# Attention's query and key projections from seven block products, weight sums by GpSimd, x loaded a second time in the merge

## The reference, cut to what matters

```
h = rms_norm(x, norm_mix)                       # 512 x 1024
proj = h @ w_in                                 # attention q, k, v; delta-rule q, k, v; gates
qa = rms_norm(q per head); ka = rms_norm(k per head); va = v      # 3 groups x 8 heads x 64
per group: dilated window attention of qa, ka, va -> output, lse
o_a = softmax over groups of lse, times the outputs
o_b = gated delta rule on (causally convolved) q, k, v
merged = sigmoid(gate_a) * (o_a @ w_branch_a) + sigmoid(gate_b) * (o_b @ w_branch_b)
x = x + merged @ w_out
```

## Time and profile before

| | |
|---|---|
| median of 3 runs | 2816.6 us |
| profiled execution | 2815.5 us |
| its span, first to last instruction | 2813.7 us |
| TensorE busy | 2726.0 us, 97% |
| VectorE, ScalarE, GpSimd busy | 46%, 21%, 0% |
| mean granted TensorE clock | 0.979 of full |
| attention, queries and keys on | 111.5 to 381 us |
| merge | 880 to 1042 us |

### The profile page before, as it was taken

The page is one execution under the profiler, slowest core; times in us unless marked ns, Lnnn a source line. Parts: engine busy times, 40 slices in busy tenths (PEclk is TensorE's granted clock), DMA queues, the critical chain, the costliest instruction groups (busy, mean ns, idle before and its releaser), DMA issues.

```text
span 2813.7 us, 29464 instructions
## 1 busy us (share of the span) xinstructions
PE 2726.0 (97%) x11558; PEld 1702.0 (60%) x11558; DVE 1282.1 (46%) x2773; ACT 580.2 (21%) x1044; POOL 0.2 (0%) x4
## 2 busy tenths in 40 slices
PE   8999989999999999999999998999999999999998
PEld 4544446676665445444444445578884484788887
DVE  1144455565552112000012585467666573777743
ACT  2145532312211001110001124221111012122201
POOL 0000000000000000000000000000000000000000
PEclk9999999999999998999999998999999999999999
DMA  4111111010011221244432220122223311222222
GB/s 184 60 60 45 53 52 44 32 45 31 31 45 60 90 82 56 92 170 171 164 119 97 75 75 1 61 83 90 79 87 119 104 49 60 77 88 90 90 90 90
DMA packets 31907, 224.74 MB, mean 80 GB/s; under 512 B 3488, under 2 KB 4128, under 8 KB 5536
## 3 DMA queue, kind: packets, MB, share of 16 engines
q1 hardware_dynamic: 30384, 219.50, 22.7%
q10 hardware_dynamic: 1392, 3.41, 0.3%
HBM read 220.80 MB, written 2.10 MB: 79 GB/s over the span
## 4 chain that ended last, share of the span: by engine, by line
PE 93%; DVE 3%; ACT 2%; issue 1%; DMA 0%; ACTq 0%; DVEq 0%
PE psum L400 91%; DVE work L2329 1%; PE psum L782 1%; PE psum L1091 0%; DVE work L709 0%; PE psum L2193 0%; PE psum L1892 0%; DVE xT L1635 0%; DVE hT L563 0%; DMA mixT<-x_dram 0%; ACT work L534 0%; PE psum L1704 0%; PE psum L3233 0%; ACT work L602 0%; ACT work L616 0%
## 5 line engine op out<-in xcount | busy, mean ns | idle before, releaser
L400 PE MATMUL psum<-hT,ring 128*128 128x512 f32 (+2 forms) x3248 | 903.3, 455 | 13.5 <-ACT work L1220 5.5
L400 PEld LDWEIGHTS psum<-hT,ring 128*128 128x128 f32 (+1 forms) x3248 | 445.7, 167 | 355.6 <-issue 324.2
L400 PE MATMUL psum<-work,ring 128*128 128x512 f32 (+1 forms) x1208 | 420.1, 499 | 8.7 <-DVE work L2391 3.9
L400 PEld LDWEIGHTS psum<-work 128*128 128x128 f32 (+2 forms) x2390 | 276.2, 178 | 113.1 <-issue 72.4
L400 PE MATMUL psum<-work 128*128 128x128 f32 (+7 forms) x2390 | 328.0, 291 | 14.3 <-ACT work L2291 11.1
L400 PEld LDWEIGHTS psum<-work,ring 128*128 128x128 f32 x1208 | 229.0, 190 | 184.7 <-issue 158.0
L400 PE MATMUL psum<-work,mixT 128*128 128x256 f32 (+2 forms) x1332 | 289.2, 379 | 2.7 <-ACT work L1745 1.5
L400 PEld LDWEIGHTS psum<-work,mixT 128*128 128x128 f32 (+1 forms) x1332 | 232.1, 182 | 49.2 <-issue 16.1
L400 PE MATMUL psum<-ring,work 128*128 (+1 forms) x568 | 247.0, 593 | 2.5 <-issue 1.9
L400 PEld LDWEIGHTS psum<-ring,work 128*128 128x128 f32 x568 | 106.7, 190 | 132.8 <-issue 129.1
L2656 DVE SCALAR_TENSOR_TENSOR work<-work,vec 128x512 f32<-128x512 f32 x176 | 125.6, 748 | 69.5 <-ACT work L2591 69.5
(11 more groups left out here) (408 smaller groups left out, 2068.1 us busy)
## 6 DMA issues: line engine op xcount, KB each, us to landing
ring<-stream_dram SPq DMA_DIRECT2D x204, 1024.0 KB, 4.8
con<-consts_dram SPq DMA_DIRECT2D x1, 2953.0 KB, 13.8
mixT<-x_dram ACTq DMA_DIRECT2D x4, 512.0 KB, 6.2
out_dram<-mixT SPq DMA_DIRECT2D x4, 512.0 KB, 3.7
work<-p_dram ACTq DMA_DIRECT2D x1, 512.0 KB, 3.9
con<-ssm_dram ACTq DMA_DIRECT2D x1, 512.0 KB, 3.5
vec<-vecs_dram SPq DMA_DIRECT2D x1, 378.0 KB, 5.5
work<-consts_dram ACTq DMA_DIRECT2D x1, 256.0 KB, 2.6
```

What stands on the lines that cost most here:

```text
L400: ins = self.eng.matmul(out, lhsT, rhs, start=start, stop=stop)
```

## The change

* Each fill's two tiles (256 output channels by 512 tokens, from 1024 input channels) are now made from seven products of blocks of 128 x 512 weights by 512 x 256 tokens, that is 28 matmuls of 256 columns in place of 16 of 512. Four sums of halves of hT are made once, by VectorE in the values stage, and kept in xT's room. Four sums of weight blocks per fill are made by GpSimd: one in a buffer of its own, three in place in the ring's slot.
* ScalarE copies three of the seven results out of PSUM, VectorE puts the two tiles together with seven additions of 256 columns, in three pieces called left, right and last; both tiles are complete only at last.
* Eleven matmuls (parts) go into each step, and the squares and head sums of both tiles of a fill come together.
* Since xT's room is taken, the turning of x moves from the values stage into the merge: x is loaded again (ScalarE's queue), and for m from 4 to 7 TensorE turns 8 blocks ahead of the gate tiles, ScalarE writes them to xT.
* ScalarE's copies of K0 and V0 move from decay_act to the end of attn_act, and TensorE's stage wait between attention and decay is dropped.
* The feed-forward's counters of h_sum start at 4 more. Nothing else of it changes.

```diff
-        TILES, AHEAD, UNITS_A, PER_STEP = 24, 6, 32, 6
+        TILES, AHEAD, UNITS_A, PER_STEP = 24, 6, 32, 11
+        SEVEN = 28
+        s_one = a(T)
+        kept = mixT[:, 0:2, :].rearrange("p a t -> p (a t)")
+        in_sums = xT[...]
+        def parts_before(n):
+            return min(SEVEN * AHEAD // 2 + PER_STEP * n, SEVEN * TILES // 2)
+        def fills_of_step(n, part):
+            at = {"left": 16, "right": 24, "last": 28}[part]
+            return [f for f in range(TILES // 2) if n >= 0 and parts_before(n) < SEVEN * f + at <= parts_before(n + 1)]
+        def fill_part_pe(e, f, i, k):            # part i of 7, k of 4
+            if k == 0:
+                if i == 0 and f >= 1: e.eng.wait_ge(S["part_read"], 7 * (f - 1) + 3)
+                if i == 1: ...; e.eng.wait_ge(S["slot_sum"], 4 * f + 1)
+                if i == 2 and f >= 1: e.eng.wait_ge(S["part_read"], 7 * (f - 1) + 7)
+                if i == 3: e.eng.wait_ge(S["slot_sum"], 4 * f + 2)
+                if i == 4: e.eng.wait_ge(S["part_out"], 2 * f + 1); e.eng.wait_ge(S["slot_sum"], 4 * f + 3)
+                if i == 5: e.eng.wait_ge(S["slot_sum"], 4 * f + 4)
+                if i == 6: e.eng.wait_ge(S["part_out"], 2 * f + 2); e.eng.wait_ge(S["part_read"], 7 * f + 1)
+            ...
+        def slot_sums_pool(e, f, fill):
+            ...                                  # waits: fill landed, part 7*(f-1)+2
+            nc.gpsimd.tensor_tensor(s_one, a21, a22, ALU.add).then_inc(S["slot_sum"], 1)
+            nc.gpsimd.tensor_tensor(a21, a11, a21, ALU.subtract).then_inc(S["slot_sum"], 1)
+            e.eng.wait_ge(S["part"], 7 * f + 1)
+            nc.gpsimd.tensor_tensor(a11, s_one, a11, ALU.subtract).then_inc(S["slot_sum"], 1)
+            e.eng.wait_ge(S["part"], 7 * f + 3)
+            nc.gpsimd.tensor_tensor(a12, a12, a11, ALU.subtract).then_inc(S["slot_sum"], 1)
+        def parts_out_act(e, f): ...             # 128x512 copy, after part 2 of the fill
+        def swap_out_act(e, f): ...              # 128x256 copy, after part 4
+        def left_dve(e, f, dst): ...             # 1 addition, after part 4 and both copies
+        def right_dve(e, f, dst): ...            # 5 additions, after part 6
+        def last_dve(e, f, dst): ...             # 1 addition, after part 7
@@ values_pe, values_act, values_dve
-                    for b in (2 * g - 2, 2 * g - 1):
-                        for half in range(2):
-                            turn_tokens_pe(e, x_tok, b, half)
+            for n, (o, in0, in1) in enumerate(...):   # four sums of halves of hT
+                nc.vector.tensor_tensor(in_sums[:, o, :, :], in0, in1, ALU.subtract).then_inc(S["h_sum"], 1)
@@ attn_pe
-                qk_products_pe(e, lo, min(lo + 2, hi))
+                qk_parts_pe(e, lo, min(lo + 4, hi))
+                for f in [AHEAD // 2 - 1] if n == 0 else fills_of_step(n - 1, "last"):
+                    head_sums_pe(e, 2 * f)
+                    head_sums_pe(e, 2 * f + 1)
+                qk_parts_pe(e, min(lo + 4, hi), hi)
@@ attn_act, per step: squares of a finished fill, turned(n), the copies of a fill with "left" in n, exps(n + 2), root
+            e.eng.wait_ge(S["mixed"], UNITS_A)
+            tile_out_act(e, 0, K0)
+            tile_out_act(e, 0, V0)
@@ attn_dve: left(0) right(0) last(0) left(1) right(1) scaled(1) last(1) left(2) scaled(3) right(2) last(2) maxima(0) ...
+                for f in [AHEAD // 2 - 1] if n == 1 else fills_of_step(n - 2, "last"):
+                    scaled(2 * f + 1)
+                left(f), right(f), last(f) of the fills of step n
@@ decay_act
-            tile_out_act(e, 0, K0)
-            tile_out_act(e, 0, V0)
@@ merge_pe, m >= 4
+                    e.eng.wait_ge(S["x_in%d" % (m - EARLY)], 32)
+                    for half in range(2):
+                        turn_tokens_pe(e, x_again, m - EARLY, half)
@@ between attention and decay on TensorE
-            e.eng.wait_ge(S["stage"], e.c["stage"].next())
+            e.c["stage"].next()
+        @block.gpsimd
+        def _(pool):
+            for f in range(TILES // 2): slot_sums_pool(e, f, fill_at["qk%d" % f])
```

More of the change, by code:

```diff
@@ L429, in program @@
         S = Sems()
+        fill_at = {}
         NF = stream.shape[0]
@@ L738, in share_bank, with qk_parts_pe, qk_half, half @@
             return psum[:, (4, 0, 1, 3)[pair], :]
-        def qk_products_pe(e, first, last):
+        def qk_parts_pe(e, first, last):
             for q in range(first, last):
[L743 to L752, removed]
+                f, r = divmod(q, SEVEN)
+                if r == 0:
+                    e.eng.wait_ge(S[e.landing()], e.landed())
+                    fill_at["qk%d" % f] = e.c["fill"].n
+                    e.fast_weights = e.slot(ring)
+                fill_part_pe(e, f, *divmod(r, 4))
+        def qk_half(f):
+            def half(tile, late):
+                t, dst = (T // 2) * late, qk_tile(2 * f + tile)
+                return residues(dst)[:, P // 2 * late:P // 2 * late + P // 2, :] if f % 3 else dst[:, t:t + T // 2]
+            return half
         def head_sums_pe(e, g):
@@ L885, in attn_act @@
             for n in range(UNITS_A):
-                g = AHEAD - 1 if n == 0 else tile_of_step(n - 1)
-                if g is not None:
-                    square(g)
+                done = [AHEAD // 2 - 1] if n == 0 else fills_of_step(n - 1, "last")
+                for f in done:
+                    square(2 * f)
+                    square(2 * f + 1)
                 turned(n)
+                for f in fills_of_step(n, "left"):
+                    parts_out_act(e, f)
+                    swap_out_act(e, f)
                 if n + 2 < UNITS_A:
                     exps(n + 2)
-                if g is not None and g % 2:
-                    root(g)
+                for f in done:
+                    root(2 * f + 1)
                 if n == UNITS_A - 2:
@@ L985, in attn_dve @@
                     shares(n + 1)
-                if n == 1:
-                    scaled(AHEAD - 1)
-                elif n >= 2 and tile_of_step(n - 2) is not None and tile_of_step(n - 2) % 2:
-                    scaled(tile_of_step(n - 2))
-                if tile_of_step(n) is not None:
-                    qk_out(tile_of_step(n))
+                for f in [AHEAD // 2 - 1] if n == 1 else fills_of_step(n - 2, "last"):
+                    scaled(2 * f + 1)
+                for f in fills_of_step(n, "left"):
+                    left(f)
+                for f in fills_of_step(n, "right"):
+                    right(f)
+                for f in fills_of_step(n, "last"):
+                    last(f)
                 if n == UNITS_A - 1:
@@ L3482, in _ @@
             ffn_dve(e, "ffn1", "f1_w", closing=True)
+        @block.gpsimd
+        def _(pool):
+            e = Engine("pool", pool, S, acc)
+            for f in range(TILES // 2):
+                slot_sums_pool(e, f, fill_at["qk%d" % f])
         @block.sync
```

169 lines of the change are left out of this document (122 added, 47 removed).

## The result

The changed kernel takes 2827.2 us (median of 9 runs, 2826.3 to 2828.4), the kernel before 2817.5 beside it (9 runs, 2812.9 to 2823.6): a ratio of 1.0036, 95% interval [1.0028, 1.0044]. It is slower by some 10 us; the forecast was 2816.4, no change. The profiled execution has a span of 2826.0 us, 12.3 more than that of before, whose profiled execution is one of its shorter ones.

A forecast was written before the change was run, and what follows sets the result against it. The prediction took TensorE, 97% busy, to bound the kernel. Attention -1.4, clock +1.7, decay -7.1 and merge +6.6 summed to -0.2 us, so it forecast a median of 2816.4 us, range 2806 to 2828.

The forecast's parts named there:

- The first turn: Ahead of the attention loop: the first turn comes at 159.2 us against 159.9, after TensorE idles 6.5 us.
- The ring: Attention loop: last, squares, head sums, root, scaled, right's bank-freeing addition; TensorE waits 2.2 to 2.5 us at fills 5, 7 and 9.
- GpSimd's sums hidden from TensorE: Attention: four weight sums a fill, about 1.2 us each by estimate, cost TensorE nothing up to 3.0 us each.
- Decay: Decay stage: early K0 and V0 copies remove 5.45 us of idle and 1.65 of slow clock, -7.1 us.
- the rival of absent waits: Attention loop: its new waits are mostly absent, 10.4 us gained, 2806 us; chance 0.22.
- Attention: Attention stage: waits of 23.2 us against 4.0, TensorE work less by 20.6, -1.4 us; +0.3 with 1.7 of clock.
- the clock term: Attention: slow clock adds 1.7 us after the idle ahead of the loop, nothing for waits under 3 us.
- -10.3 and +10.4: Attention loop: 10.3 us of TensorE work removed up to step 22, against 10.4 us of new waits.
- nothing for waits under 3 us: Attention loop: short waits lower no clock, 0 us; upper bound 1.7 at each of five long waits.
- GpSimd in VectorE's way: Attention loop: sums delay VectorE's operations with two SBUF inputs, +9 us, 2825 us, deciding from 1.2 us a sum; chance 0.18.
- Merge: Merge: turning x adds transposes and bank waits on TensorE, 1.65 us four times, +6.6 us (bounds 3.4 and 8).
- The clock was a rival of the prediction: Attention loop: the clock falls at five waits of 2 to 3.5 us, 1.7 each, +8, 2824 us; chance 0.12.

The follow-up runs named there:

- e_early: Kernel before with only ScalarE's K0 and V0 copies moved into attention and TensorE's stage wait dropped: 2810.9 us, ratio 0.9964.
- e_before_1: Kernel before plus one idle 512-column product ahead of the merge's last product group: 2821.8 us, ratio 1.0018.
- e_after_3: Changed kernel plus three idle 512-column products ahead of the merge's last product group: 2825.9 us, ratio 1.0033 to the kernel before.
- experiment 4: Changed kernel with VectorE's scaled behind right and last: 2823.4 us, ratio 1.0019; also without GpSimd's sums: 2821.2 us, 1.0009.
- experiment 8: Both kernels rerun (2817.6, 2828.3 us), then idle products before the merge's last group: kernel before 2821.8, changed 2825.9, kernel before with copies moved 2809.4.

## Why the prediction was wrong

**The steps that held.** The first turn at 160.0 us (forecast 159.2). The ring: the waits on right's second addition, four times and 6.9 us in all, the first large one 2.07 us at 224.0 (forecast 2.2 at 218.9); all waits of the loop that the view names 9.7 us (forecast 10.4). GpSimd's sums hidden from TensorE: 1.28 us each in the mean (1.26 to 1.47), near the 1.2 estimated from the Trainium skill (GPSIMD Engine Reference, 3.1). Decay: -7.1, shown alone by e_early. So the queues of VectorE and ScalarE eat most of what the seven products save, as forecast; the rival of absent waits is refuted.

**Attention: +5.4 instead of +0.3.** Without the clock it is +0.8 (+0.5 in the second run of each), where the terms gave -1.4; the clock is +4.6 (+4.3), where the sum had 1.7. This is the first place where the sum failed: the clock term, put at 1.7 ahead of the loop and at nothing behind shorter waits. By stretches. Up to the first turn 48.0 us against 48.6, the -0.7 of the forecast. First to second turn +3.1 (10.7 against 7.6): one head sum more falls in (0.9), 0.4 of products less, and 6 us at a clock of 0.56 lose 2.6, where the term "1.7 for the 6.5 us ahead of the loop" stood: 0.9 off. Second turn to step 23 +4.6 (174.3 against 169.7), where the terms were -10.3 and +10.4. A step without waits takes 6.78 us against 7.18, so 22 of them save 8.8; a stretch of half clock at 305.3 us, which began as a wait of 2.33 us ended, costs 1.7, where "nothing for waits under 3 us" stood (of the four long waits on right's second addition it is the only one with half clock behind it); the rest is 11.7, of which the waits are 9.7; that the other 2 are the stop and start around each wait is not shown. From there to the end it is -1.6, although the 3.84 us wait is followed by 6.8 us of half clock, where before has 3.4 at that point; the 2.2 us wait forecast for step 24 did not come.

**GpSimd in VectorE's way.** The rival was right in kind and two to three times too large: 3.4 us (4.4 by the attention stage) instead of 9. The sum is 1.28 us, past the point of 1.2 from which it was to decide. What failed is the share of meetings: the rival let a third of scaled and right's two-input operations meet a sum, but none of right's 36 such additions did, and of scaled's 36 instances one was held. What is held is mostly what the prediction did not count, the one-input multiplications of shares and of the negated maxima.

**Merge: +7.6 instead of +6.6.** The mechanism was right: with banks of its own 3.5 us are left, which are the transposes (forecast 3.4), and the two shared banks cost 4.1, where the terms 0.5 and 0.2 four times gave 2.8 and a rounding.

**Behind the merge: +7.5 instead of 0.** This is the step that failed most. The sum has no term for the stages behind the merge, and weighs the clock only where TensorE stops. (Its own walk of the kernel before had found some 2 us of half clock late in attention, where TensorE hardly stops.) The same work ran at half clock for 10 us more in the router; e_before_1 and e_after_3 show that the point at which the merge ends does this, and that it makes up 2.7 to 4.0 of the 7.5 us. The clock was a rival of the prediction, at +8, but for the waits inside the loop; of attention's +4.6 it gave 1.7 there, and the larger part of the whole came where no edit and no new wait was. Why the chip grants less at one position than at another is open: the runs show the dependence, not the cause.

Added up without the clock, the forecast had attention -1.4, decay -5.5 (7.1 without the 1.65 of slow clock), merge +6.6, in all -0.3; the traces have +0.8, -6.6, +7.6 and 1.4 in the stages that no edit touches, in all +3.2, as the runs have it. That alone is 0.11%, inside the 0.2% at which no change was forecast; the +6.1 of the clock, forecast at 0 (1.7 and -1.65), made it slower. So the forecast of no change failed by its clock term and not by its walk of the queues, whose net was off by 2.2 us in attention, within the 3 us that it allowed itself. That near hit is in part luck: the loop's waits were smaller than forecast (13.8 us instead of 16.1 from the first turn on), and time around them that had no term took it back.

## What to carry to other kernels

Where TensorE is 97% busy, removed products come back as waits once the queues behind them carry more; walk these queues before believing the arithmetic, and put the instructions that free a bank ahead of those that don't (here 3 us at full clock). Test the parts of a compound change one by one: the smallest edit here was the only one that paid, 7 us. And a change of a few microseconds shifts all that follows against the granted clock: compare span times granted clock, the half clock of each stage while TensorE is busy, and the length of untouched stages, before reading a difference of 0.3% as the work of an edit.

## What the runs showed of the hardware

* A VectorE instruction that reads only SBUF and starts while a GpSimd sum of two SBUF tiles runs ends 0.02 to 0.55 us after the sum, whatever its size: 128 x 2 from 0.17 to 1.01 us, 128 x 256 from 0.35 to 1.4, a 64 x 512 scalar_tensor_tensor from 0.75 to 1.67 (at 140.5 us), a 128 x 512 tensor_tensor from 0.69 to 1.01 (L1072, at 226.9 us). It need not have two inputs, and having them is no cure. A memset (7 instances of L1042 beside a sum, all 0.06 us), a reciprocal of two columns (6, all under 0.16 us) and whatever reads PSUM were never held. The Trainium skill (SBUF — State Buffer, "Who interferes with whom") has both: two SBUF inputs contend, and a tensor_scalar in a mode that takes both port pairs contends too; the trace agrees. The prediction had read only the first half.
* A GpSimd addition or subtraction of 128 x 512 fp32 takes 1.28 us in the mean, where VectorE takes 0.69 for one in SBUF (L1072, alone).
* Half clock fell on stages with TensorE busy nearly throughout (14.91 of 15.00 us at a clock of 0.66, experiment 4), and at the 3 us gaps of the values stage in some executions (at 50.0, 84.1 and 114.9 us in the second run of the changed kernel), where the earlier trace rows had none.
* The same stage of the same code had 20.5, 23.9 or 30.7 us of half clock according to where it lay in time (experiment 8).
